# Cross attention with the query weights multiplied by the keys first, and half the columns per level in delta attention's block inverse

## What is computed

```python
def cross_attention(h, m, w_q, w_kv, w_o):
    q = einsum('bsd,de->bse', h, w_q)              # 512 x 2048
    k, v = split(einsum('bmd,de->bme', m, w_kv))   # 256 x 2048 each
    scores = einsum('bshd,bmhd->bhsm', q, k) * 512 ** -0.5
    o = einsum('bhsm,bmhd->bshd', softmax(scores), v)
    return einsum('bse,ed->bsd', o, w_o)
```

```python
    sol = triangular_solve(eye + lower, rhs, left_side=True, lower=True, unit_diagonal=True)
```

## Time and profile before

| | |
|---|---|
| median of 3 runs | 3012.13 us (3011.26 to 3015.68) |
| the profiled execution, its own time | 3020.96 us |
| its span | 3019.1 us |
| busy: PE, PEld, DVE, ACT, POOL | 98%, 81%, 53%, 34%, 15% |
| mean granted TensorE clock | 0.99 of full speed |
| HBM read, written | 362.05 MB, 81.79 MB |

### The profile page before, as it was taken

The page is one execution under the profiler, slowest core; times in us unless marked ns, Lnnn a source line. Parts: engine busy times, 40 slices in busy tenths (PEclk is TensorE's granted clock), DMA queues, the critical chain, the costliest instruction groups (busy, mean ns, idle before and its releaser), DMA issues.

```text
span 3019.1 us, 36826 instructions
## 1 busy us (share of the span) xinstructions
PE 2944.8 (98%) x14210; PEld 2441.8 (81%) x14210; DVE 1615.0 (53%) x1560; ACT 1035.4 (34%) x1115; POOL 441.8 (15%) x461
## 2 busy tenths in 40 slices
PE   7999999989999999999999999999999999999997
PEld 6777877777778998888788788888888788888886
DVE  5443766655434452342444443333333688888888
ACT  6222333333334332231333332232323333333334
POOL 3000111100001113300010223233332300000001
PEclk9999999999999999999999999999999999999999
DMA  7333222222325874434423255555555765555555
GB/s 241 88 87 90 71 60 59 57 60 80 105 77 147 246 239 131 120 110 129 139 99 99 85 166 193 172 185 180 177 187 170 263 252 208 208 208 204 203 204 133
DMA packets 484927, 447.59 MB, mean 148 GB/s; under 512 B 15598, under 2 KB 404848, under 8 KB 483952
## 3 DMA queue, kind: packets, MB, share of 16 engines
q1 hardware_dynamic: 453520, 346.25, 38.1%
q0 software_dynamic: 31328, 100.25, 9.2%
HBM read 362.05 MB, written 81.79 MB: 147 GB/s over the span
## 4 chain that ended last, share of the span: by engine, by line
PE 89%; DVE 4%; DMA 3%; ACT 2%; issue 2%; POOL 0%; SPq 0%; DVEq 0%; ACTq 0%; POOLq 0%
PE slab_ps L851 19%; PE slab_ps L852 19%; PE slab_ps L853 19%; PE down_ps L1392 6%; PE down_ps L1394 6%; PE down_ps L1393 6%; PE mix_ps L1263 1%; PE down_ps L851 1%; PE down_ps L853 1%; PE mix_ps L852 1%; PE down_ps L852 1%; PE mix_ps L851 1%; PE mix_ps L853 1%; DVE w_lo L1988 1%; DMA w_raw<-in_w_in_dram 1%
## 5 line engine op out<-in xcount | busy, mean ns | idle before, releaser
L851 PE MATMUL slab_ps<-act_hi,w_hi 128*128 128x512 f32 (+1 forms) x2960 | 1128.1, 381 | 8.7 <-DVE w_lo L1988 4.0
L852 PE MATMUL slab_ps<-act_lo,w_hi 128*128 128x512 f32 (+1 forms) x2960 | 1102.1, 372 | 0.0
L853 PE MATMUL slab_ps<-act_hi,w_lo 128*128 128x512 f32 (+1 forms) x2960 | 1102.0, 372 | 0.0
L851 PEld LDWEIGHTS slab_ps<-act_hi,w_hi 128*128 128x128 f32 x2960 | 560.7, 189 | 114.7 <-issue 14.6
L853 PEld LDWEIGHTS slab_ps<-act_hi,w_lo 128*128 128x128 f32 x2960 | 559.9, 189 | 97.7
L852 PEld LDWEIGHTS slab_ps<-act_lo,w_hi 128*128 128x128 f32 x2960 | 560.8, 189 | 95.2 <-issue 5.5
L1988 DVE TENSOR_TENSOR w_lo<-w_raw,w_hi 128x2048 fp32r<-128x2048 f32 x200 | 468.7, 2344 | 311.7 <-ACT w_hi L1418 311.4
L1418 ACT ACTIVATE w_hi<-w_raw 128x2048 fp32r<-128x2048 f32 x200 | 382.1, 1910 | 609.0 <-PE slab_ps L853 575.5
L1392 PE MATMUL down_ps<-half_hi,u_slot 128*128 128x512 f32 x896 | 350.4, 391 | 3.0 <-DMA u_slot<-u_park 2.3
L1394 PE MATMUL down_ps<-half_lo,u_slot 128*128 128x512 f32 x896 | 350.2, 391 | 0.0
L1393 PE MATMUL down_ps<-half_hi,u_slot 128*128 128x512 f32 x896 | 349.9, 391 | 0.0
(11 more groups left out here) (385 smaller groups left out, 2680.4 us busy)
## 6 DMA issues: line engine op xcount, KB each, us to landing
w_raw<-in_w_mlp_up_dram SPq DMA_DIRECT2D x64, 1024.0 KB, 6.6
b<-in_w_mlp_down_dram SPq DMA_DIRECT2D x64, 1024.0 KB, 6.9
w_raw<-in_w_in_dram SPq DMA_DIRECT2D x56, 1024.0 KB, 5.6
u_slot<-u_park SPq DMA_DIRECT2D x112, 512.0 KB, 8.8
w_raw<-in_w_cross_kv_dram SPq DMA_DIRECT2D x32, 1024.0 KB, 6.5
u_park<-u_hi POOLq DMA_DIRECT2D x32, 896.0 KB, 6.6
u_park<-u_lo POOLq DMA_DIRECT2D x32, 896.0 KB, 7.8
w_raw<-in_w_mix_out_dram SPq DMA_DIRECT2D x16, 1024.0 KB, 6.0
```

The costliest lines, as they stand in the source:

```text
L851: mm(ps, wh, xh, start=first, stop=False)
L852: mm(ps, wh, xl, start=False, stop=False)
L853: return mm(ps, wl, xh, start=False, stop=last)
```

## The change

Two edits. Edit 1, cross attention: the scores are (h W_q) K^T; now W_q,head K_head^T is made first, a 2048 x 256 matrix per head, and the activations are multiplied by that. The query weights arrive transposed. The heads are done in two halves (p = 0, 1) of two heads (hh) each. For each half there are four j of two `keys_window` (one per head: 48 fp32r matmuls of 256 columns, four 128-row tiles t of the product over four slices d) and, one j later, one `scores_block` (48 fp32r matmuls of 512 columns, both heads side by side, into banks M[0] to M[3]). The products are taken out of PSUM as a high part (ACT) and a low part (DVE) into the space of `vo_hi` and `vo_lo`; keys are split as well (`key_hi`, `key_lo`), and both halves' keys are loaded in one transfer each. The norm (`crs`) now enters as the scale of the exponential. Softmax of both heads of a half is done at once: the first half's beside the second half's keys windows, the second half's beside the value windows. `turn_weights` runs once per half, after `values_window(1)` and `values_window(2)`.

Edit 2, the block inverse: all matmuls of levels 1 to 6, ScalarE's copy and VectorE's subtractions work on the 64 of 128 columns per tile that change (strided access, `halves_of`). At the last level the V product has 64 output rows, so its weights have 64 columns. Because `dn_uu` is also used whole as weights, POOL clears it before each copy but the last (`dn_zero`), and POOL's mask of level n now waits for V of level n - 2, not for U.

```diff
+        def halves_of(t, n, which):
+            return t.rearrange("p (b two h) -> p b two h", two=2, h=2 ** n)[:, :, which, :]
...
-            matrix(w_cq_v, KT)
+            with sp.Fori(0, 2) as i:
+                slabs.enter(i, 2 * NT)
+                for j in range(NT):
+                    for hh in range(2):
+                        load(w_cqt_v[:, bass.ds(i * 2 + hh, 1), :, j * S:(j + 1) * S].rearrange("p a d n -> p (a d) n"))
+            slabs.leave(2)
...
                         if n >= 3:
-                            pool.wait_ge(on["dn_u"], hd * 6 + (n - 2))
+                            pool.wait_ge(on["dn_v"], hd * 6 + (n - 2))
...
+                        if n == 0 or n >= 3:
+                            nc.gpsimd.memset(dn_uu[:], 0.0).then_inc(on["dn_zero"], 1)
...
+            pool.dma_start(k_raw0[:], k_park[0:2 * NH].rearrange("k p m -> p k m")).then_inc(kv_loaded[0], 16)
...
-                        last = mm(tile(M[2], c), tile(dn_ctt[:, n % 2], c), tile(dn_xx, c), start=True, stop=True)
+                        last = mm(halves_of(tile(M[2], c), n, 0), tile(dn_ctt[:, n % 2], c),
+                                  halves_of(tile(dn_xx, c), n, 0), start=True, stop=True)
...
-                            mm(tile(M[3], c), tile(dn_xt, c), tile(dn_uu, c), start=True, stop=True)
-                        last = mm(tile(M[4], c), tile(dn_uu, c), tile(dn_xt, c), start=True, stop=True)
+                            mm(halves_of(tile(M[3], c), n, 0), tile(dn_xt, c), halves_of(tile(dn_uu, c), n, 0), start=True,
+                               stop=True)
+                        rows = slice(0, P if n < 6 else P // 2)
+                        last = mm(halves_of(tile(M[4], c), n, 1)[rows], tile(dn_uu, c)[:, rows],
+                                  halves_of(tile(dn_xt, c), n, 1), start=True, stop=True)
...
+            def keys_window(p, j, hh):
+                slot = slabs.first % 2
+                pe.wait_ge(on["key_lo"], p + 1)
+                pe.wait_ge(on["slab_lo"], slabs.at(1))
+                pe.wait_ge(on["slab_out"], slabs.at(-1))
+                wh, wl = (w[:, slot].rearrange("p (d n) -> p d n", d=NH) for w in (w_hi, w_lo))
+                for t in range(NT):
+                    for d in range(NH):
+                        last = hi_lo(quads(down_ps[3 * slot][:])[:, t], tile(wh[:, d], t), tile(wl[:, d], t),
+                                     k_hi[p][:, NH * hh + d], k_lo[:, NH * hh + d], d == 0, d == NH - 1)
...
+            def scores_block(p, j):
...
+                for k in range(NT * j, NT * (j + 1)):
...
+                    for t in range(NT):
+                        last = hi_lo(M[t][:], tile(act_hi[:, k], t), tile(act_lo[:, k], t), vo_hi[:, i], vo_lo[:, i],
+                                     k == 0, k == KT - 1)
...
+            for p in range(2):
+                for j in range(NT):
+                    for hh in range(2):
+                        keys_window(p, j, hh)
+                    if p == 0 and j == 0:
+                        token_totals()
+                    if j > 0:
+                        scores_block(p, j - 1)
+                scores_block(p, NT - 1)
...
             values_window(0, new_act=True)
-            head_scores((NH - 1) % 2, NH - 1)
             values_window(1, new_act=True)
+            turn_weights(0)
             values_window(2, new_act=True)
-            turn_weights(NH - 1)
+            turn_weights(1)
             values_window(3, new_act=True)
...
-                    fn(dn_uu[:], M[2][:], ACT.Copy).then_inc(on["dn_uev"], 1)
+                    if n < 6:
+                        act.wait_ge(on["dn_zero"], hd * 5 + n)
+                    fn(halves_of(dn_uu[:], n, 0), halves_of(M[2][:], n, 0), ACT.Copy).then_inc(on["dn_uev"], 1)
...
+            def scores_hi(j, hh):
+                slabs.step()
+                split_hi()
+                act.wait_ge(on["slab_mul"], slabs.at())
+                fn(product_part(vo_hi, j, hh), quads(down_ps[3 * (1 - slabs.first % 2)][:]), ACT.Copy).then_inc(
+                    on["vo_hi"], 1)
...
                     if n < 6:
-                        chain.put(tt(dn_xx[:], dn_xx[:], M[3][:], ALU.subtract))
-                    tt(dn_xt[:], dn_xt[:], M[4][:], ALU.subtract).then_inc(on["dn_x"], 1)
+                        xx = halves_of(dn_xx[:], n, 0)
+                        chain.put(tt(xx, xx, halves_of(M[3][:], n, 0), ALU.subtract))
+                    rows = slice(0, P if n < 6 else P // 2)
+                    xt = halves_of(dn_xt[:], n, 1)[rows]
+                    tt(xt, xt, halves_of(M[4][:], n, 1)[rows], ALU.subtract).then_inc(on["dn_x"], 1)
```

More of the change, by code:

```diff
@@ L1254, in _ @@
             tile = lambda t, c: t[:, c * P:(c + 1) * P]
-            def head_scores(par, hd):
-                pe.wait_ge(on["slab_out"], slabs.at())
-                pe.wait_ge(on["cx_done"], hd + 2)
-                pe.wait_ge(kv_loaded[par], 16 * (hd // 2 + 1))
-                for st in range(NT):
-                    for k in range(NH):
-                        last = mm(M[st // 2][:, (st % 2) * NMEM:(st % 2 + 1) * NMEM], tile(cstage[:, par, k], st),
-                                  kh[:, par, k], start=k == 0, stop=k == NH - 1)
-                last.then_inc(on["cx_scores"], 1)
@@ L1267, in turn_weights @@
-            def turn_weights(hd):
-                pe.wait_ge(on["cx_p"], hd + 1)
-                for st in range(NT):
-                    for mt in range(MT):
-                        last = nc.tensor.transpose(tile(M[2 + mt], st), prob[:, st, mt * P:(mt + 1) * P], ident[:])
-                last.then_inc(on["cx_pt"], 1)
-            def attention(par, hd):
-                head_scores(par, hd)
-                for _ in range(9):
-                    yield HOP
-                turn_weights(hd)
-                for _ in range(4):
-                    yield SEG
@@ L1284, in _ @@
-            window(total(1), new_act=True)
-            for _ in range(3):
-                window()
-            for hd in range(NH - 1):
-                mixer = attention(hd % 2, hd)
-                for n in range(4):
-                    window(mixer, last_use=hd == NH - 2 and n == 3)
+            def keys_window(p, j, hh):
[8 more added lines that the diff above has]
+                                     k_hi[p][:, NH * hh + d], k_lo[:, NH * hh + d], d == 0, d == NH - 1)
+                last.then_inc(on["slab_mul"], 1)
+                slabs.step()
@@ new lines, in token_totals, with turn_weights @@
+            def token_totals():
+                pe.wait_ge(on["xacc_ready"], KT)
+                for t in range(NT):
+                    last = mm(tile(M[0], t), tile(xacc, t), ones[:], start=True, stop=True)
+                last.then_inc(on["x_total"], 1)
+            def turn_weights(p):
+                pe.wait_ge(on["cx_p"], p + 1)
+                if p == 0:
+                    pe.wait_ge(on["cx_exp"], 4)
+                else:
+                    pe.wait_ge(on["pt_ready"], MT * NH // 2)
+                for i in range(MT * 2):
+                    for t in range(NT):
+                        last = nc.tensor.transpose(tile(M[i], t), tile(prob[:, p, t], i), ident[:])
+                last.then_inc(on["cx_pt"], 1)
@@ L2468, in residual @@
                     split_lo()
+                    if m == KT // 2:
+                        key_lo(0)
                     slabs.step()
[L2471 to L2479 removed]
@@ new lines, in scores_lo, with head_max @@
+            def scores_lo(n, j, hh):
+                split_lo()
+                dve.wait_ge(on["vo_hi"], n + 1)
+                dve.wait_ge(on["slab_mul"], slabs.at())
+                tt(product_part(vo_lo, j, hh), quads(down_ps[3 * (1 - slabs.first % 2)][:]),
+                   f32(product_part(vo_hi, j, hh)), ALU.subtract).then_inc(on["slab_out"], 1)
+            def head_max(p, n):
+                dve.wait_ge(on["cx_scores"], p + 1)
+                both = slice(2 * n, 2 * n + 2)
+                for t in range(2 * n, 2 * n + 2):
+                    chain.put(v.tensor_reduce(ccols[:, 0, t], halves(M[t][:]), AX.X, ALU.max))
+                chain.sync()
+                stt(out=ccols[:, 1, both], in0=ccols[:, 0, both], scalar=-1.0,
+                    in1=crs[:, 1, both].unsqueeze(2).broadcast_to([P, 2, 2]), op0=ALU.mult, op1=ALU.mult).then_inc(
+                    on["cx_max"], 1)
```

219 lines of the change are left out of this document (120 added, 99 removed).

## The result

The changed kernel took 2986.68 us (median, 2985.79 to 2987.34) beside 3013.9 (3011.26 to 3019.27): a ratio of 0.9907, 95% interval 0.9895 to 0.992. The forecast was 2983.0. The profiled execution took 2987.21, its span 2985.2.

A forecast was written before the change was run, and what follows sets the result against it. TensorE, busy 98% of the span, was taken as the bound, so time is a sum over matmuls. Gains of 24.8 and 4.3 make 29.1 us: 2991.9 from the profiled 3020.96, 2983.0 in the median's terms; range 2955 to 2993.

The forecast's parts named there:

- the 29.1 of the sum: Whole change: 24.8 us gained in cross attention plus 4.3 in the block inverse.
- Columns of edit 1: Cross attention: keys windows 92.2 and scores blocks 87.0, together 179.2 us against 203.1 for query windows and fp32 scores.
- Start: First keys windows of cross attention: activation split wanted only 24 us later, so it costs nothing.
- Exit: Before the second turn_weights: TensorE waits 2.2 us for VectorE's splits, and a lower clock costs 1.6 more.
- Handover: Four keys windows in a row, second half: splits and eviction take 5.4 against 5.76 us; 0.5 charged.
- the rival with 2999: Cross attention: keys windows wait for their split, one us each for 16, giving 2999; chance 0.05.
- Load-bound matmuls: Block inverse levels: 64-column matmuls stay 0.11 us apart, nothing gained; the stream-bound rival gains 28, giving 2955, chance 0.13.
- V to U at levels 3 and 4: Block inverse: halved VectorE subtractions remove TensorE's wait of 0.32 us, at two levels of four heads, 2.6 in all.
- Last level, 1.7: Block inverse, last level: 32 records load 64 columns, 0.054 us less each, 1.7 gained.
- The clear: POOL's clear of dn_uu, 0.5 us, covered by 1 us at U(3); late-clear rival gives 2992, chance 0.12.
- Slower by the clock: Rival: half-empty streams in 24 level blocks lower the granted clock, costing 38 us, giving 3021; chance 0.04.

The follow-up runs named there:

- `start_order`: Changed kernel with VectorE's last residual add and slab split moved ahead of the last four activation tiles; 2988.88 us, ratio 0.9901.
- `e1_only`: Cross attention edit alone: the changed kernel with the old block inverse; 2994.84 us, ratio 0.9922.
- `exit_order`: Changed kernel with VectorE splitting the first four turned tiles before the second value product, not after; 2986.58 us, ratio 0.99.
- `cols16`: Changed kernel with only 16 of the 64 columns streamed in each level product; 2992.11 us in its one execution.
- `no_clear`: Changed kernel without POOL's clear, level products and ScalarE's copy at full width, subtractions halved, last V weights 64 columns; 2989.85 us, ratio 0.9909.
- `e1_again`: Second profiled execution of `e1_only`, unchanged; 2988.47 us, span 2987.0.
- `e2_only`: Block inverse edit alone: the kernel before with the new block inverse; 3012.95 us, ratio 0.9986.
- `slow_clear`: Changed kernel with each POOL clear four times as large (2048 columns, 512 of them dn_uu); 3013.82 us, ratio 0.9989.

## Why the prediction came out

The total was right, partly by luck, since two sets of errors lie under it: terms of the sum were too large, and some 2 us of clock that it did not count made up for a part. The second profile of before gives a pair without the falls at the heads' ends: 3010.1 and 2985.1 (the changed kernel again), 25.0 us. The medians are 27.2 apart in the first comparison and 29.2 in the last, since executions of the kernel before fall to the lower clock more often: the mean granted clock of its runs is mostly 0.990 to 0.992, that of the changed kernel's 0.992 to 0.994. At the same mean clock, 0.993, five runs of before took 3011.9 to 3012.8 and four of the changed kernel 2986.3 to 2987.3: some 25.5. So the edits give some 25, and 2 to 4 go with the clock, which the forecast did not count and which no run ties to an edit. Against 25 stand the 29.1 of the sum. Of the 25.0 of the pair, 22.7 lie in the stretch of the first edit and 0.8 in the delta heads; the other 1.5 lie in pieces under 0.6 elsewhere, and no run says what they are.

- **Columns of edit 1.** Right: keys matmuls at 0.120, and with the fp32 scores gone the stretch falls by 22.5 (234.65 to 212.18; 22.7 in the second pair) where 24.8 was forecast. Of the difference of 2.4, the next two terms are 1.6 and 0.4; the other 0.4 stands in no wait.
- **Start.** "The activation split is wanted only by the first scores block, 24 us later: nothing." That step failed. The activation split is not wanted, but it stands in VectorE's queue before work that is: 1.59 us, shown by `start_order`. The question was asked of the result and not of the queue.
- **Exit.** Forecast 2.2 and 1.6 for the clock, measured 2.54 and 1.7, in both executions of the changed kernel; without the fall in both of `e1_only`. The cause is the order on VectorE, as `exit_order` shows.
- **Handover.** 0.5 forecast, 0.40 measured. Beyond this and the one at the start no keys window waited: the rival with 2999 did not happen.
- **Load-bound matmuls.** Right, and `cols16` settles it.
- **V to U at levels 3 and 4.** Right to the digit. From the window matmul ahead of U(3) to the one behind it: 350.35 to 351.71, 1.36 us, in the second profile of before, and 350.39 to 351.43, 1.04, in the second of the changed kernel. 0.32 at eight places is 2.6, and it is VectorE's shorter subtraction, since `no_clear` with full streams has 1.04 too.
- **Last level, 1.7.** Mis-sized. The eight narrow loads are as short as forecast (0.54 together), but the first of them starts only when the window matmul before has streamed (0.36 us of idle, the third wait in the list above), and the first window load of full shape starts only with its own matmul at 374.38. From 373.45 to 374.38 it is 0.93; in the second profile of before the same eight records take this:

```profile
374.05 0.39 PE L853 MATMUL slab_ps<-act_hi,w_lo 128*128 128x512 f32 x1
...
374.28 1.05 PE L1038 MATMUL mix_ps<-dn_xt,dn_uu 128*128 128x128 f32 x8
...
375.09 0.48 PE L851 MATMUL slab_ps<-act_hi,w_hi 128*128 128x512 f32 x1
```

1.04. So 0.1 for each head and at most 0.4 in all, not 1.7.
- **The clear.** "Covered, by 1 us" was right for U(3), and no wait of ScalarE on POOL reached TensorE. But at level 1 the wait for VectorE grew from 1.7 to 3.5, so the clear costs 1.8. The forecast asked who waits for POOL and not whom POOL holds up.

Edit 2 by these: 2.6 + 0.4 - 1.8 = 1.2 us, where 4.3 was forecast. The traces give rather less. From the first wait of the heads (`dn_rows`) to the last head's last state product it is 326.24 to 615.11, 288.87 us, in the second profile of before, 325.83 to 614.63, 288.80, in `e1_again`, which has the old inverse too, and 325.81 to 613.90, 288.09, in the second profile of the changed kernel: 0.7 to 0.8. Further on the difference of the two kernels looks larger, but 0.4 of it was there before the heads (326.24 and 325.81): the first matmul behind the last head (`gla_qk`) starts at 643.61 and 642.40, the first query or keys matmul at 1278.24 and 1276.48. `e2_only` has 4.2 in its median, which looks like the forecast and is not it: its runs at a mean clock of 0.993 took 3009.6 to 3010.5, against 3011.9 to 3012.8 for the kernel before at the same: about 2.

- **Slower by the clock.** Did not happen: half-width streams brought no fall at the levels, and `e2_only` had two at the heads' ends where before had four, then none. `cols16`, with 16 columns, had one at a level, in the first head and not in the other three. The changed kernel has another fall, at 628 to 634 us in both of its profiles (0.50 from 630 to 632), which neither profile of before has. It costs nothing: behind it TensorE waits for VectorE (`gla_qk`), 3.4 us instead of 5.00, and from the last state product to that matmul it is 28.50 us in the second profiles of both kernels:

```profile
642.38 1.14 PE L1147 MATMUL mix_ps<-gla_qk 64*128 64x256 f32 x8 [3.43 <-DVE gla_qk L2357]
```

## What to carry to other kernels

For work that "nobody wants yet", look where it stands in its engine's queue and what is wanted behind it; the two large waits of the first edit were of that kind, and moving one step for each took 3.3 and 1.2 us out of the trace, too little for the medians to show. Work put on POOL is costed by whom it holds up, and VectorE operations with all operands in SBUF come first. Before a difference of a few us is read from a pair of profiles, take a second profile of the same kernel: here 9.0 us lay between two executions. And follow a difference back to where it begins: 0.4 of the 1.2 us that seemed to be the second edit's stood ahead of its first instruction.

## What was not expected of the hardware

- A stall of up to 1.9 us is followed by the lower clock in one execution and not in the next of the same kernel, at four places at once (windows above).
- An fp32 matmul of 16 columns comes no sooner than one of 128: 0.112 us, the load.
- Going from 128x128 weights to 128x64 and back leaves a load uncovered on each side: it took back at least 1.3 of the 1.7 us that the narrower loads save. With full streams of 128 columns (`no_clear`) the same place takes 1.34 us instead of 1.04, a loss:

```profile
372.63 0.39 PE L869 MATMUL slab_ps<-act_hi,w_lo 128*128 128x512 f32 x1
372.95 1.09 PE L1055 MATMUL mix_ps<-dn_xt,dn_uu 128*64 128x128 f32 x8
373.97 0.50 PE L867 MATMUL slab_ps<-act_hi,w_hi 128*128 128x512 f32 x1
```

- A POOL multiply with a clear of 1.81 us right behind it stretched a VectorE operation from 0.48 to 2.69 us, with a clear of 0.52 to 1.41: VectorE did not get its turn between the two. An operation with an operand in PSUM kept its 0.42, beside the multiply (above) and beside a clear (at 343.44 us of `slow_clear`, with a clear from 342.37 to 344.19).
- A fall of the clock ahead of a wait for another engine cost nothing: the wait became shorter by 1.6 us (5.00 to 3.43).
